# A ring of six instead of eight gather slots in the expert layers of a hybrid decoder step

## What is computed

```python
def peer_ffn(xn, w_q, sub_keys, u_tab, v_tab):
    q = (x2 @ w_q).reshape(T, PEER_HEADS, 2, PEER_HALF)          # 8 heads, two halves of 128
    s = einsum('thpd,hpnd->thpn', q, sub_keys)
    sv, si = top_k(s, 16)                                         # of 128 keys, each half
    cand, cidx = all 16 x 16 sums and their expert numbers
    top_s, top_i = top_k(cand, 16)                                # 16 experts a head
    idx  = ...reshape(T, 128)                                     # 128 experts for a token
    gate = softmax(top_s).reshape(T, 128)
    h = einsum('td,ted->te', xb, u_tab[idx])                      # D_MODEL = 1024
    act = gelu(h) * gate
    return einsum('te,ted->td', act, v_tab[idx])
```

## Time and profile before

| | |
|---|---|
| median of 2 runs | 4751.18 us (4749.53 to 4752.84) |
| the profiled execution | 4759.28 us |
| its span in the profile | 4757.5 us |
| the loop of `peer` in layer 0 | 929.8 to 2436 us of the span |
| the loop of `peer` in layer 1 | 3247 to 4748 us of the span |

### The profile page before, as it was taken

One profiled execution on the slowest core, in us unless ns is written; L12 is line 12 of the kernel. 1 busy time (PEld: TensorE's weight loads), 2 busy tenths in 40 slices (PEclk: granted clock), 3 DMA queues, 4 the chain that ended last, 5 costly groups with the idle time before them and its releaser, 6 DMA issues. The chain is left out here.

```text
span 4757.5 us, 44863 instructions
## 1 busy us (share of the span) xinstructions
PE 3197.3 (67%) x15751; PEld 1465.6 (31%) x15751; DVE 2496.4 (52%) x6121; ACT 520.0 (11%) x1186; POOL 1152.0 (24%) x1188
## 2 busy tenths in 40 slices
PE   7977787378566566556568777864776566565665
PEld 6867673235011111111123465543331111111111
DVE  3423441556666566566534433225666665765764
ACT  2212230110000000000012322110100000000000
POOL 0002330023333333333300010002333333333332
PEclk8987888689666666676679888887886666766766
DMA  2220001499999999999941034236999999999997
GB/s 90 71 64 23 2 1 68 144 390 402 372 380 371 375 375 377 380 384 372 375 159 52 0 155 176 77 109 278 378 397 376 377 380 375 382 377 369 383 377 309
DMA packets 214920, 1248.90 MB, mean 263 GB/s; under 512 B 31512, under 2 KB 51232, under 8 KB 79200
## 3 DMA queue, kind: packets, MB, share of 16 engines
q0 software_dynamic: 152448, 1133.58, 60.8%
q1 hardware_dynamic: 62304, 113.20, 7.0%
HBM read 1232.44 MB, written 7.86 MB: 261 GB/s over the span
## 5 line engine op out<-in xcount | busy, mean ns | idle before, releaser
L1310 DVE SCALAR_TENSOR_TENSOR ring<-ring,bc 128x1024 f32<-128x1024 f32 x1040 | 1268.9, 1220 | 1055.6 <-PE bc L1329 800.5
L1261 POOL DMA_INDIRECT ring<-in_uv,idxT x1040 | 996.7, 958 | 2435.4 <-PE acc L1342 1713.8
L1329 PE MATMUL bc<-xb,sel 96*128 96x512 bf16 x2080 | 843.5, 497 | 1048.4 <-DVE ring L1310 1048.1
L1342 PE MATMUL acc<-ring,st 128*32 128x512 f32 x4160 | 854.5, 939 | 44.9 <-DVE st L1295 42.8
L1329 PEld LDWEIGHTS bc<-xb,sel 96*128 96x128 bf16 x2080 | 135.9, 104 | 1811.3 <-DVE ring L1310 1514.7
L1342 PEld LDWEIGHTS acc<-ring,st 128*32 128x32 f32 x4160 | 155.3, 153 | 600.1 <-issue 344.6
L1275 ACT ACTIVATE hg<-hs 128x4 f32<-128x4 f32 x260 | 53.4, 205 | 2365.6 <-DVE ring L1310 2365.6
L1213 PE MATMUL side<-xnT,w 128*128 128x128 f32 (+1 forms) x1536 | 258.6, 320 | 32.1 <-DMA w<-in_w_peer 30.2
L1213 PEld LDWEIGHTS side<-xnT,w 128*128 128x128 f32 x1536 | 219.1, 195 | 87.2 <-DMA w<-in_w_peer 47.7
L269 PE MATMUL acc<-xnT,w 128*128 128x260 f32 x1024 | 228.5, 385 | 5.1 <-ACT inp L305 4.2
L269 PEld LDWEIGHTS acc<-xnT,w 128*128 128x128 f32 x1024 | 195.3, 191 | 38.0 <-ACT inp L305 6.6
(11 more groups left out here) (436 smaller groups left out, 3675.1 us busy)
## 6 DMA issues: line engine op xcount, KB each, us to landing
w<-in_w_peer SPq DMA_DIRECT2D x96, 512.0 KB, 8.1
ring<-in_uv,idxT POOLq DMA_INDIRECT x1040, 9.6
w<-in_w_gdn SPq DMA_DIRECT2D x32, 512.0 KB, 3.4
xb<-pieces SPq DMA_DIRECT2D x96, 64.0 KB
S<-in_state_ssm SPq DMA_DIRECT2D x16, 256.0 KB, 3.1
out_ssm_s<-S SPq DMA_DIRECT2D x16, 256.0 KB, 3.2
w<-in_w_gdn_out SPq DMA_DIRECT2D x2, 2048.0 KB, 13.5
w<-in_w_mla_out SPq DMA_DIRECT2D x2, 2048.0 KB, 13.4
```

The source lines that it names most:

```text
L1261: pool.indirect_dma_start(out=ring[:, n % RING, :], out_offset=None, in_=core.i[f"uv{layer}"], in_offset=bass.IndirectOffsetOnAxis(ap=idxT ...
L1310: dve.scalar_tensor_tensor(ring[:, n % RING, 0:D], ring[:, n % RING, 0:D], 1.0, bc[:, :], ALU.mult, ALU.mult, accum_out=hs[:, k % 2, c:c + ...
L1329: last = pe.matmul(bc[:, HALF * e:HALF * e + HALF], sel[:, r:r + 1].to_broadcast([PIECES * 32, P]), xb[b % 2][:, g, HALF * e:HALF * e + HA ...
L1342: last = pe.matmul(acc[32 * g:32 * g + 32, HALF * e:HALF * e + HALF], st[:, k % 2, c, :], ring[:, n % RING, D + HALF * e:D + HALF * e + HA ...
```

## The change

```diff
--- before.py
+++ after.py
@@ -52,7 +52,7 @@
 EPS = 1e-6
 ROPE_THETA = 10000.0
 NEG = -1.0e30
-RING = 8
+RING = 6
```

## The result

The changed kernel takes 5741.8 us (median of 2 runs, 5734.1 to 5749.5) against 4751.2: the ratio is 1.208, with an interval of 1.205 to 1.211. The forecast was 5705 us. The profiled execution of after took 5734.1 us with a span of 5732.3, which is 974.8 us more than the span of before.

The account below looks back on a forecast made before the run. The prediction took the `peer` loops as just bound by transfers; six slots close the circle in one group, 15.0 us against 11.22. At 477 us a layer, 954 for both, it forecast 5705 us, range 5400 to 5930.

Parts of the forecast that it names:

- The circle over one group: In the `peer` loops, a group's values release the second gather the next group needs: 15.0 us a group against 11.22.
- Its terms: One turn: release 0.31, second gather's landing after first issue 8.75, dot 1.22, last dot to values' end 4.47 us.
- the clock: TensorE's granted clock falls as the same work spreads over more time, lengthening the values: 0.25 us a group.
- The landing: Second gather of a released four lands 8.75 us after the first's issue, taken between 8.1 and 9.3.
- the last term: End of a group's last dot to end of its values (gelu, gates, spread, value matmuls): 4.47 us.
- block 0: First 32 groups of a layer's loop, where SP's loads share the DMA engines: 498 us against 393, +105.
- the tail: Last two groups of a layer, the sample tokens, whose gathers now wait: 42.6 us against 34, +9.
- A: Gathers land sooner, the second 8.15 us after the first's issue: 13.7 us a group, 5363 us; chance 0.12.
- B: Two gathers travel side by side, the second landing at 6.75 us: 12.75 us a group, 5115 us; chance 0.04.
- D: Every step of the turn at its long end, landing at 9.3: 16.2 us a group, 6035 us; chance 0.07.
- C: Loop stays bound by transfers, two gathers in flight bridge the release: price nothing, 4751 us; chance 0.03.
- step 2: In the turn, first issue to landing of the second gather, on an empty queue: 8.75 us.

Follow-up runs that it names:

- run 1: Changed kernel with the tile back at eight slots and only the wait at six: 5733.7 us, 15.19 us a group.
- run 2: Changed kernel with seven slots in place of six: 4977.9 us, ratio 1.046 to the kernel before.
- run 3: Changed kernel, six slots in the tile, but each gather waits for the group of the token five earlier: 6377.4 us.
- run 5: Changed kernel (six slots) with the upper-512-column value matmuls left out for most prompt groups: 5449.3 us.
- run 4: Kernel before with nine slots in place of eight: 4693.1 us, ratio 0.988.
- run 6: Kernel before (eight slots) with the upper-512-column value matmuls left out for most prompt groups: 4589.3 us, against 4763.3 on the same chip.
- run 10: Kernel before with nine slots, gates and spread ahead of the thread steps, value matmuls cut in two halves: 4552.2 us, ratio 0.956.

## Why the prediction was right

- **The circle over one group, closed by the second gather.** Right, and shown from three sides: the wait alone gives the whole loss (run 1), a shift of the wait by one gather either way gives the steps 12.06, 15.19 and 17.64 (runs 2 and 3), and a shorter term of the circle comes off a turn (run 5: 1.26 of 1.45 us).
- **Its terms.** Forecast 0.31 + 8.75 + 1.22 + 4.47, and 0.25 for the clock, 15.0. Measured in blocks 1 to 3: 0.31 + 8.99 (8.60 to the last completion record, 0.39 more to the dot) + 1.22 + 4.64 = 15.16, beside 15.19 from batch to batch. The landing, taken as the middle of two values, was 0.24 longer; the last term with the clock was 0.08 shorter than its 4.72. The clock cost 0.13 of the 0.25 (values 3.47 in place of 3.34; granted clock 0.61 in place of 0.66).
- **The sum.** Forecast for a layer: 363 for blocks 1 to 3, 105 for block 0, 9 for the tail, 477 in all. Measured in layer 0: 1462 - 1077 = 385, 492 - 393 = 99, and 5 for what is left of 489; in layer 1, 484 as a whole. So blocks 1 to 3 were 22 us over, 0.23 a group, and the two small terms 10 under. For the profiled execution the forecast was 5713 us, and it took 5734.1, 21 more. The other 16 of the 37 us between 5705 and 5741.8 are no term of the kernel: the forecast put the median 8 us under the profiled execution, as it was before, and it came 8 over it.
- **The signs.** POOL held 258 times for 10.5 us (forecast 256 to 258 times, 10.4), 277 GB/s (280), DMA share 0.72 and clock 0.61 (under 0.97, under 0.65) came as told. The second of each four is used 7.75 us after its issue (7.5), and DVE's wait for the broadcast fell from 800 to 626 us. DVE's wait for gathers rose to 1390 us, where "600 or more" was said.
- **Rivals.** A and B (5363 and 5115 us) needed a second landing at 8.15 or 6.75; it was 9.0. D (6035 us) had that landing nearly right with 9.3 and overrated the rest. C needed a landing at 5.2 and is out: a turn costs what it costs with an empty queue.
- **The Trainium skill's rule on step 2.** The fit that the Trainium skill gives ("DMA: Bandwidth & Descriptors", section "Anatomy of one DMA — SWDGE (gpsimd) path") makes an estimate of 4.4 us for such a transfer, and by it the prediction's sum would have been 12.8 us a group. The measured 15.2 speaks against its use for an indirect gather of 8 KB rows, whose dot starts 5.67 us after its issue on an empty queue.
- **What was wrong, though it cost nothing here.** The prediction called the 11.22 us of before "near the floor" of the transfers. Runs 4, 6 and 10 show that it was not: the same bytes go through in 10.31 us a group. With nine slots, where the gathers are there in time, a group still takes 10.85. So the kernel before was held mostly by the chain of DVE and PE, and the ring of eight added 0.35 to it. The gather that comes close there is the first of a four: its dot starts 0.65 us after its last completion record (median), where the three others have 1.75 us or more.

## What to carry to other kernels

Where one group's work frees buffers for a later one, write down which transfer of the released batch the next group can't end without, and add up one turn with an empty queue: release, issue, landing, use, release. That sum, divided by the groups it spans, is a bound as hard as the bandwidth, and it moves in steps when a slot is taken, not in proportion. Where it spans one group it gave the time itself (12.05 for 12.06, 15.16 for 15.19). Where it spans two it was only a lower bound: with eight slots and the fourth gather, (0.31 + 14.0 + 1.22 + 4.64) / 2 = 10.1 us, an estimate from the records of after, lies under the measured 11.20, since the chain of DVE and PE takes longer. So add up that chain too and take the longest. A DMA share near 1 doesn't tell the two apart; GB/s against the best stretch, and a run with one slot more, do.

## What the runs showed of the hardware that was not expected

- In a batch of four gathers of 1.05 MB, the first dot that waits starts 5.67 us after the first issue and the second 3.50 later (timeline of after), while a third costs only 2.45 more (runs 1 and 3). So the gap between the first two landings is more than one transfer at the later rate. Part of it lies in stragglers: by the single records of after, the eighth of the sixteen completions comes at 4.90, 7.60, 10.14 and 12.63 us after the first issue, the last at 5.32, 8.62, 11.12 and 13.64. What makes them late was not settled.
- The first gather of a batch lands about as soon with one transfer still under way (5.45 us, run 2) as with an empty queue (5.3 us in after, both by the single records). With more still under way it lands later: 6.9 us in the kernel before, where the last of the four before it lands 3.5 us after its issue.
- The DMA share stood at 0.97 to 1.01 over stretches that moved 376, 388 and 409 GB/s.
